# Masking the turned attention probabilities: four VectorE products on the unsplit values, or eight GpSimd products on the two rounded parts

## The chip, the cores and the metric

The kernel runs on one core of one Trainium2 chip. The metric is the device time of one execution in microseconds (us). The engines of a core work beside each other, each through its own list of instructions in order, and meet at semaphores: TensorE (PE) multiplies matrices into PSUM, VectorE (DVE) and ScalarE (ACT) do elementwise work on SBUF and PSUM, GpSimd (POOL) does elementwise work on SBUF, and SyncE (SP) issues transfers.

## The reference, cut to what matters

One decoder layer on 2048 tokens of 1024 channels. A normalised input is projected once into 50 column tiles of 128. One group of columns feeds a short convolution, the other feeds sliding-window attention with 16 heads of 64 in blocks of 128 queries; both are gated, joined, projected back and added to the input. The part that the change touches is the product of the probabilities and the values. A block of queries sees its own 128 keys and the block before, but within a window of 128 in all:

```python
    dist = BLOCK + qi[:, None] - kj[None, :]
    valid = ((dist >= 0) & (dist < WINDOW))[None, :, :] & (key_pos >= 0)[:, None, :]
    ...
    scores = jnp.where(valid[None, :, None, None], scores + alibi[None, None], -jnp.inf)
    ...
    p = jnp.exp(scores - m)
    denom = jnp.sum(p, axis=-1, keepdims=True) + jnp.exp(sink - m)
    probs = (p / denom).astype(v.dtype)
    out = jnp.einsum("bnhgqk,bnkhd->bnqhgd", probs, v_band)
```

So each query has exactly 128 valid keys out of 256: key column k belongs either to the query's own block (k at or before the query) or to the block before it (k after the query). The two sets of valid places are two triangles that fill one 128 x 128 square.

## The kernel before

**Tiles.** The 2048 tokens are two halves of 1024. Within a half, after the key and value columns, a loop runs over 8 tiles of channels; a tile holds two attention heads and 128 convolution channels. A tile has six weight tiles (Q, C, U, B, GC, GA), each multiplied with two chunks of 512 tokens: 12 jobs of 24 matmuls (L1260), since every fp32 operand is split in a rounded part ("hi") and a rest ("lo") and three of the four products are made. There are 16 tiles in all (8 in each half). Behind them comes the output projection (L1427).

**Units.** The attention of a tile is done in 4 units (u = 0 to 3) of two blocks of queries and two heads. Through a unit the work runs so:

- PE `scores(u)` (L1350) into `score_bank`.
- DVE `maxima(u)` (L1009 to L1020): adds the bias, takes row maxima, and folds the two key blocks of a query into one 128 x 128 square by a maximum (L1015), since each place has one valid value only. It begins by waiting for `pT_ready` of unit u-2 (for u = 0: of the unit just before).
- ACT `exps(u)` (L688, L692), DVE `denominators(u)` (L1026, L1028), POOL `normalise(u)` (L512).
- PE `turn(u)` (L1363): four 128 x 128 transposes into `turn_bank`.
- DVE `pT_rest(u)` and ACT `pT_round(u)`: four products of the turned square with the two triangles of `in_block` (L1036) unfold it back into the two key blocks, in the SBUF tile `probs` under its other name `parted`; ACT rounds each query block to `pT_hi` (L701); DVE subtracts to get `pT_lo` (L1042) and signals `pT_ready`.
- PE `weigh(u)` (L1377): 8 matmuls of the values with `pT_hi` and `pT_lo`. It waits for all of `pT_ready` of its unit.
- ACT `shift(u)` (L708, L709) and DVE `attn_out(u)` (L1055) take the result from `out_bank` to `attn_y`.

**Order.** Every engine's order is written out by hand. PE's order in a tile is: Q0, Q1, scores 0, C0, C1, scores 1, U0, turn 0, U1, scores 2, B0, weigh 0, turn 1, GC0, scores 3, GA0, weigh 1, turn 2, B1, GC1, weigh 2, turn 3, GA1, weigh 3. So between turn(u) and weigh(u) stand two jobs for u = 0, 1 and 2, but one (GA1) for u = 3.

DVE's order behind turn(0) is: convolve(0), pT_rest(0), the split of a weight tile (L822), maxima(2), denominators(2), times_b(0) (L1081), convolve(1), attn_out(0), pT_rest(1), gate(GC,0) (L1089), apply_gate (L1097), maxima(3), denominators(3), gate(GA,0), attn_out(1), apply_gate, pT_rest(2), times_b(1), a weight split, gate(GC,1), apply_gate, a weight split, attn_out(2), pT_rest(3), gate(GA,1), attn_out(3), apply_gate. POOL's order in a tile is `normalise` 0 to 2, the squares of the convolution result (`add_squares`, L519 and L522, two instructions each), normalise(3), and three more `add_squares`.

## Time and profile before

| | |
|---|---|
| median of 3 runs | 1688.5 us (1688.47 to 1691.25) |
| profiled execution, span | 1689.7 us |
| PE busy | 1638.5 us, 97% |
| DVE busy | 1038.0 us, 61% |
| ACT busy | 560.3 us, 33% |
| POOL busy | 267.0 us, 16% |

The span is the time from the first to the last instruction of one profiled execution; it lies inside the spread of the runs and 1.2 us above their median. Busy shares are averages over the whole run. In the tile loops they hide that an engine with a low share can still end a wait; what a change there is worth is read from one tile's timeline, and the tiles repeat.

### The profile page before, as it was taken

Reading aid. Unit: us, or ns where it says so; the run is one execution under the profiler, and the core shown is the slowest. Engines: PE = TensorE matmul, PEld = TensorE weight load, DVE = VectorE, ACT = ScalarE, POOL = GpSimd, SP = SyncE. Lnnn points to the kernel's source line nnn. Section 1 sums busy time; section 2 is a strip of 40 time slices with the busy share of each in tenths; the row PEclk is TensorE's granted clock in tenths of the full one; section 3 lists DMA queues with packets and bytes.
Section 4 is the critical chain, followed back from the end, with each engine's and each line's share of the span. In section 5 each row is a group of like instructions: output and inputs, shape, how many; then the busy total and the mean of one; then the engine's idle time right before and its main releaser. Section 6 shows DMA issues by size and latency. Waiting matters only on the chain.

```text
span 1689.7 us, 23074 instructions
## 1 busy us (share of the span) xinstructions
PE 1638.5 (97%) x7824; PEld 1370.7 (81%) x7824; DVE 1038.0 (61%) x2262; ACT 560.3 (33%) x1275; POOL 267.0 (16%) x229
## 2 busy tenths in 40 slices
PE   5999999999999998999999999999999899999996
PEld 4888888888888886788888888888888688888885
DVE  6376767667576758567667676766667643333332
ACT  6333433343333354333333333333333421111110
POOL 1021212122121302112122121312122000000000
...
DMA packets 61774, 125.42 MB, mean 74 GB/s; under 512 B 4640, under 2 KB 37408, under 8 KB 59680
## 3 DMA queue, kind: packets, MB, share of 16 engines
...
## 4 chain that ended last, share of the span: by engine, by line
PE 84%; DVE 8%; issue 3%; ACT 3%; DMA 1%; SPq 0%; DVEq 0%; POOL 0%; ACTq 0%; POOLq 0%
PE job_bank L1260 57%; PE job_bank L1427 8%; PE score_bank L1427 5%; PE turn_bank L1427 5%; PE score_bank L1350 3%; PE out_bank L1377 3%; PE out_bank L1427 2%; DVE probs L1036 1%; PE turn_bank L1363 1%; DVE w_lo L822 1%; DVE hT_lo L857 1%; DVE tanh_sb L1089 1%; DVE pT_lo L1042 1%; ACT pT_hi L701 1%; DVE attn_y L1055 1%
## 5 line engine op out<-in xcount | busy, mean ns | idle before, releaser
L1260 PE MATMUL job_bank<-hT_hi,w_hi 128*128 128x512 f32 x1600 | 635.4, 397 | 9.9 <-DVE conv_y L1081 4.5
L1260 PE MATMUL job_bank<-hT_lo,w_hi 128*128 128x512 f32 x1600 | 627.7, 392 | 0.0
L1260 PE MATMUL job_bank<-hT_hi,w_lo 128*128 128x512 f32 x1600 | 627.7, 392 | 0.0
L1260 PEld LDWEIGHTS job_bank<-hT_hi,w_hi 128*128 128x128 f32 x1600 | 302.9, 189 | 70.2 <-issue 6.0
L1260 PEld LDWEIGHTS job_bank<-hT_hi,w_lo 128*128 128x128 f32 x1600 | 302.6, 189 | 65.5
L1260 PEld LDWEIGHTS job_bank<-hT_lo,w_hi 128*128 128x128 f32 x1600 | 303.2, 190 | 58.5
L512 POOL TENSOR_TENSOR probs<-probs,smax 128x512 f32<-128x512 f32 x64 | 66.6, 1040 | 795.6 <-DVE smax L1028 795.6
L688 ACT ACTIVATE probs<-probs,smax 128x128 f32<-128x128 f32 x256 | 99.8, 391 | 253.4 <-DVE smax L1020 253.4
L822 DVE TENSOR_TENSOR w_lo<-w_raw,w_hi 128x1024 fp32r<-128x1024 f32 x100 | 122.4, 1224 | 87.1 <-ACT w_hi L558 84.3
L701 ACT ACTIVATE pT_hi<-probs 128x512 fp32r<-128x512 f32 x128 | 80.7, 633 | 258.7 <-DVE probs L1036 257.0
L558 ACT ACTIVATE w_hi<-w_raw 128x1024 fp32r<-128x1024 f32 x100 | 105.3, 1053 | 0.8
L793 ACT ACTIVATE wo_raw<-z 128x1024 f32<-128x1024 f32 x16 | 17.0, 1061 | 255.8 <-DVE z L1226 255.8
L1009 DVE CUSTOM_DVE_ANT_0 probs<-score_bank,bias 128x256 f32<-128x256 f32 x256 | 93.0, 420 | 0.7 <-DVE tanh_sb L1089 0.2
L1036 DVE TENSOR_TENSOR probs<-turn_bank,in_block 128x256 f32<-128x256 f32 x256 | 90.8, 418 | 2.0
L1042 DVE TENSOR_TENSOR pT_lo<-probs,pT_hi 128x512 fp32r<-128x512 f32 x128 | 86.8, 696 | 6.8 <-ACT pT_hi L701 4.1
L1026 DVE TENSOR_TENSOR smax<-smax 128x4 f32<-128x4 f32 x64 | 10.4, 163 | 114.2 <-ACT smax L692 114.2
L1427 PE MATMUL job_bank<-wo_early,mix_hi 128*128 128x512 f32 x256 | 69.8, 395 | 7.2 <-DVE wo_early L887 7.2
L1350 PEld LDWEIGHTS score_bank<-keys,qs 128*128 128x128 f32 x512 | 69.5, 188 | 5.5
L1089 DVE SCALAR_TENSOR_TENSOR tanh_sb<-tanh_sb,job_bank 128x512 f32<-128x512 f32 x64 | 43.9, 686 | 46.0 <-ACT tanh_sb L719 44.4
L1226 DVE SCALAR_TENSOR_TENSOR z<-job_bank,mix_r,z 128x512 f32<-128x512 f32 x24 | 17.3, 748 | 87.6 <-PE score_bank L1427 86.6
L1350 PE MATMUL score_bank<-keys,qs 128*128 128x256 f32 x512 | 70.9, 280 | 0.0
L519 POOL TENSOR_TENSOR square<-attn_y 128x512 f32<-128x512 f32 x32 | 40.5, 1267 | 171.2 <-DVE attn_y L1055 171.2
...
## 6 DMA issues: line engine op xcount, KB each, us to landing
...
```

What stands on the lines that cost most here:

```text
L512: nc.gpsimd.tensor_tensor(merged, merged, smax[:, u % 2, ROWSUM, :].unsqueeze(2).to_broadcast([P, 4, BLOCK]), ALU.mult).then_inc(probs_rea ...
L558: nc.scalar.activation(w_hi[:, slot], w_raw[:, slot], ACT.Copy).then_inc(w_hi_ready, 1)
L688: nc.scalar.activation(probs[:, u % 2, c // 2, c % 2, 0:BLOCK], probs[:, u % 2, c // 2, c % 2, 0:BLOCK], ACT.Exp, bias=smax[:, u % 2, NEGM ...
L701: nc.scalar.activation(pT_hi[:, b, :], parted[:, u % 2, b].rearrange("p k h q -> p (k h q)"), ACT.Copy).then_inc(pT_hi_ready, 1)
L822: nc.vector.tensor_tensor(w_lo[:, slot], w_raw[:, slot], w_hi[:, slot].bitcast(F32), ALU.subtract).then_inc(w_ready, 1)
L1009: ins = nc.vector.tensor_tensor_reduce(probs[:, u % 2, h, b, :], score_bank[h][:, b, :], bias[:, first, h, :], 1.0, MASKED, ALU.add, ALU.m ...
L1036: ins = nc.vector.tensor_tensor(parted[:, u % 2, b, kb], turned.rearrange("p (h q) -> p h q", h=2), in_block[:, kb].unsqueeze(1).to_broadc ...
L1042: nc.vector.tensor_tensor(pT_lo[:, b, :], parted[:, u % 2, b].rearrange("p k h q -> p (k h q)"), pT_hi[:, b, :].bitcast(F32), ALU.subtract ...
L1089: nc.vector.scalar_tensor_tensor(out=tanh_sb[:, ch, :], in0=tanh_sb[:, ch, :], scalar=1.0, in1=job_bank[slot][:], op0=ALU.add, op1=ALU.mul ...
L1260: ins = nc.tensor.matmul(job_bank[bank][:], w[:, slot, kt, :], h[:, kt, cols], start=(kt == 0 and n == 0), stop=(kt == KT - 1 and n == 2))
L1350: ins = nc.tensor.matmul(score_bank[h][:, b, :], qs[:, h, blk * BLOCK:(blk + 1) * BLOCK], keys[:, g, part, blk * BLOCK:(blk + 2) * BLOCK], ...
L1427: ins = nc.tensor.matmul(mix_bank[p][s][h], m[:, p, kt, :], wo_part(kt, part)[:, h * CHUNK:(h + 1) * CHUNK], start=(kt % TILES == 0 and n ...
```

## The change

On POOL, a function `part(u)` is new. On ACT, `pT_round(u)` no longer waits for masked values: it waits for the transposes and rounds the unmasked square of both query blocks in one instruction, from `turn_bank` into the first 256 columns of each block of `pT_hi`. On DVE, `pT_rest(u)` is one subtraction, `turn_bank` minus the rounded part, into the same columns of `pT_lo`, and it signals the new `pT_lo_ready`. POOL then waits for that and makes eight products of 128 x 256: for each query block and each of the two parts first the upper triangle into the second 256 columns (signalled by `pT_own`), then, in place, the other triangle onto the first 256 columns, with `pT_ready` behind the last two pairs. All who wait for `pT_ready` (weigh, turn and the start of maxima) thus wait for POOL. Nothing is moved on PE.

```diff
@@ -165,11 +165,11 @@
         gains = sb("gains", [P, 2, TILES])
 
 
-        parted = probs[:].rearrange("p u h b k -> p u (h b k)").rearrange(
-            "p u (b k h q) -> p u b k h q", b=UNIT_BLK, k=2, h=2)
         x_first = [x_sb[:, 0, :], x_sb[:, 1, :]] + [b[:].rearrange("p a b -> p (a b)") for b in (conv_y, gated, c_sb)] + [
             probs[:, i].rearrange("p h b k -> p (h b k)") for i in range(2)] + [
             cu[:, 0:D_MODEL]]
+        hi_parts = pT_hi[:].rearrange("p b (k h q) -> p b k h q", k=2, h=2)
+        lo_parts = pT_lo[:].rearrange("p b (k h q) -> p b k h q", k=2, h=2)
         vT = tanh_sb
         dist = w_raw[:, 2, 0:2, :].bitcast(I32)
         ROWMAX, MAX, NEGMAX, SINKDIFF, ROWSUM, SINKEXP = range(6)
@@ -252,7 +252,8 @@
         rinv_ready = sem("rinv_ready")
         probs_ready = sem("probs_ready")
         probs_turned = sem("probs_turned")
-        masked = sem("masked")
+        pT_lo_ready = sem("pT_lo_ready")
+        pT_own = sem("pT_own")
         pT_hi_ready = sem("pT_hi_ready")
         pT_ready = sem("pT_ready")
         pv_done = sem("pv_done")
@@ -522,18 +523,39 @@
                         nc.gpsimd.tensor_tensor(total[:, ch, :], total[:, ch, :], square[:],
                                                 ALU.add).then_inc(squares_step, 1)
 
+                    def part(u):
+
+                        pool.wait_ge(pT_lo_ready, unit_no(hf, it, u) + 1)
+                        for b in range(UNIT_BLK):
+                            for parts in (hi_parts, lo_parts):
+                                ins = nc.gpsimd.tensor_tensor(
+                                    parts[:, b, 1], parts[:, b, 0].bitcast(F32),
+                                    in_block[:, 1].unsqueeze(1).to_broadcast([P, 2, BLOCK]), ALU.mult)
+                            ins.then_inc(pT_own, 1)
+                        for b in range(UNIT_BLK):
+                            pool.wait_ge(pT_own, 2 * unit_no(hf, it, u) + b + 1)
+                            for parts in (hi_parts, lo_parts):
+                                ins = nc.gpsimd.tensor_tensor(
+                                    parts[:, b, 0], parts[:, b, 0].bitcast(F32),
+                                    in_block[:, 0].unsqueeze(1).to_broadcast([P, 2, BLOCK]), ALU.mult)
+                            ins.then_inc(pT_ready, 1)
+
                     normalise(0)
                     normalise(1)
+                    part(0)
                     normalise(2)
 
                     pool.wait_ge(evacuated[job_slot(hf, it, B, 0)], evac_count(hf, it, B, 0))
                     add_squares(conv_y, ssq_conv, 0, 0)
+                    part(1)
                     normalise(3)
 
                     pool.wait_ge(attn_ready, unit_no(hf, it, 1) + 2)
                     add_squares(attn_y, ssq_attn, 0, 1)
+                    part(2)
                     pool.wait_ge(evacuated[job_slot(hf, it, B, 1)], evac_count(hf, it, B, 1))
                     add_squares(conv_y, ssq_conv, 1, 2)
+                    part(3)
                     pool.wait_ge(attn_ready, unit_no(hf, it, 3) + 2)
                     add_squares(attn_y, ssq_attn, 1, 3)
 
@@ -695,11 +717,10 @@
                     def pT_round(u):
 
                         act.wait_ge(pv_done, unit_no(hf, it, u) + 1)
-                        for b in range(UNIT_BLK):
-
-                            act.wait_ge(masked, 2 * unit_no(hf, it, u) + b + 1)
-                            nc.scalar.activation(pT_hi[:, b, :], parted[:, u % 2, b].rearrange("p k h q -> p (k h q)"),
-                                                 ACT.Copy).then_inc(pT_hi_ready, 1)
+                        act.wait_ge(probs_turned, unit_no(hf, it, u) + 3)
+                        nc.scalar.activation(pT_hi[:, :, 0:2 * BLOCK],
+                                             turn_bank[u % 2][:].rearrange("p (b c) -> p b c", b=UNIT_BLK),
+                                             ACT.Copy).then_inc(pT_hi_ready, 1)
 
                     def shift(u):
 
@@ -1029,19 +1050,11 @@
 
                     def pT_rest(u):
 
-                        dve.wait_ge(probs_turned, unit_no(hf, it, u) + 3)
-                        for b in range(UNIT_BLK):
-                            turned = turn_bank[u % 2][:, 2 * b * BLOCK:2 * (b + 1) * BLOCK]
-                            for kb in range(2):
-                                ins = nc.vector.tensor_tensor(
-                                    parted[:, u % 2, b, kb], turned.rearrange("p (h q) -> p h q", h=2),
-                                    in_block[:, kb].unsqueeze(1).to_broadcast([P, 2, BLOCK]), ALU.mult)
-                            ins.then_inc(masked, 1)
-                        for b in range(UNIT_BLK):
-                            dve.wait_ge(pT_hi_ready, 2 * unit_no(hf, it, u) + b + 1)
-                            nc.vector.tensor_tensor(pT_lo[:, b, :],
-                                                    parted[:, u % 2, b].rearrange("p k h q -> p (k h q)"),
-                                                    pT_hi[:, b, :].bitcast(F32), ALU.subtract).then_inc(pT_ready, 1)
+                        dve.wait_ge(pT_hi_ready, unit_no(hf, it, u) + 1)
+                        nc.vector.tensor_tensor(pT_lo[:, :, 0:2 * BLOCK],
+                                                turn_bank[u % 2][:].rearrange("p (b c) -> p b c", b=UNIT_BLK),
+                                                pT_hi[:, :, 0:2 * BLOCK].bitcast(F32), ALU.subtract
+                                                ).then_inc(pT_lo_ready, 1)
 
                     def attn_out(u):
 
```

On POOL, behind the second normalisation of a tile, there stand before:

```order
L512 TENSOR_TENSOR probs<-probs,smax 128x4x128 [waits rinv_ready]
L529 REGISTER_ALU
L518 ISA [waits evacuated1]
L519 TENSOR_TENSOR square<-conv_y 128x512 [waits squares_step]
L521 REGISTER_ALU
L522 TENSOR_TENSOR ssq_conv<-ssq_conv,square 128x512 [waits squares_step]
```

The row at L512 is normalise(2), and the squares of the convolution follow it. In the changed kernel, from part(0) to normalise(2), with rows that repeat left out:

```order
L531 TENSOR_TENSOR pT_hi<-pT_hi,in_block 128x256 [waits pT_lo_ready]
L531 TENSOR_TENSOR pT_lo<-pT_lo,in_block 128x256
...
L536 ISA
L538 TENSOR_TENSOR pT_hi<-pT_hi,in_block 128x256 [waits pT_own]
L538 TENSOR_TENSOR pT_lo<-pT_lo,in_block 128x256
L536 REGISTER_ALU
...
L511 REGISTER_ALU
L513 TENSOR_TENSOR probs<-probs,smax 128x4x128 [waits rinv_ready]
```

Eight products now stand ahead of normalise(2), and as many ahead of normalise(3), and ahead of and behind the second squares of the convolution.

On DVE, behind the first convolution of a tile, there stand before (the last row is the first instruction of maxima(2)):

```order
L1036 TENSOR_TENSOR probs<-turn_bank,in_block 128x256 [waits probs_turned,dve_step]
L1036 TENSOR_TENSOR probs<-turn_bank,in_block 128x256 x3
L1041 REGISTER_ALU
L1042 TENSOR_TENSOR pT_lo<-probs,pT_hi 128x512 [waits pT_hi_ready] x2
L821 REGISTER_ALU
L822 TENSOR_TENSOR w_lo<-w_raw,w_hi 128x1024 [waits w_hi_ready]
L1002 REGISTER_ALU [waits probs_turned,scores_done,bias_set]
L1009 ISA probs,smax<-score_bank,bias 128x256 [waits pT_ready]
```

In the changed kernel the same place is:

```order
L1054 TENSOR_TENSOR pT_lo<-turn_bank,pT_hi 128x2x256 [waits pT_hi_ready,dve_step]
L842 REGISTER_ALU
L843 TENSOR_TENSOR w_lo<-w_raw,w_hi 128x1024 [waits w_hi_ready]
L1023 REGISTER_ALU [waits probs_turned,scores_done,bias_set]
L1030 ISA probs,smax<-score_bank,bias 128x256 [waits pT_ready]
```

Six instructions have become one. The wait of maxima for `pT_ready` stands where it stood; its signal came from two rows further up on the same engine and now comes from POOL.

## Rows read from the trace of the kernel before

**Rows 1.** The page, part 1: engine, busy us (share), instructions.
```profile
PE 1638.5 (97%) x7824; PEld 1370.7 (81%) x7824; DVE 1038.0 (61%) x2262; ACT 560.3 (33%) x1275; POOL 267.0 (16%) x229
```

**Rows 2.** Busy times over one tile: stretch, length, engines, clock, DMA share, GB/s.
```profile
326.00:401.30 75.30, 75.21 (x370) 63.23 (x369) 52.20 (x120) 26.73 (x70) 15.69 (x12) 1.00 0.17 56
```

**Rows 3.** PE's timeline: start us, us, instruction; first matmuls of weigh 0 to 3.
```profile
325.92 0.28 PE L1377 MATMUL out_bank<-pT_hi,vals 128*128 128x256 f32 x1
...
339.22 0.28 PE L1377 MATMUL out_bank<-pT_hi,vals 128*128 128x256 f32 x1
...
351.53 0.28 PE L1377 MATMUL out_bank<-pT_hi,vals 128*128 128x256 f32 x1
...
358.16 0.39 PE L1260 MATMUL job_bank<-hT_hi,w_lo 128*128 128x512 f32 x1
358.63 0.39 PE L1377 MATMUL out_bank<-pT_hi,vals 128*128 128x256 f32 x1
...
401.23 0.28 PE L1377 MATMUL out_bank<-pT_hi,vals 128*128 128x256 f32 x1
```

**Rows 4.** Waits of the weight loads: us in total, times, longest us.
```profile
PEld out_bank L1377 <- DVE pT_lo L1042: 7.1, 14, 0.5
```

**Rows 5.** DVE's timeline in the same tile, at the places that the change touches.
```profile
318.02 1.42 DVE L1036 TENSOR_TENSOR probs<-turn_bank,in_block 128x256 f32<-128x256 f32 x4
...
321.09 1.23 DVE L822 TENSOR_TENSOR w_lo<-w_raw,w_hi 128x1024 fp32r<-128x1024 f32 x1 [0.26 <-ACT w_hi L558]
322.23 0.42 DVE L1009 CUSTOM_DVE_ANT_0 probs<-score_bank,bias 128x256 f32<-128x256 f32 x1
...
333.06 1.42 DVE L1036 TENSOR_TENSOR probs<-turn_bank,in_block 128x256 f32<-128x256 f32 x4
...
337.37 0.42 DVE L1009 CUSTOM_DVE_ANT_0 probs<-score_bank,bias 128x256 f32<-128x256 f32 x1
...
344.14 1.51 DVE L1097 SCALAR_TENSOR_TENSOR gated<-attn_y,gains,tanh_sb 128x512 f32<-128x512 f32 x1 [0.24 <-DVE attn_y L1055]
345.68 1.42 DVE L1036 TENSOR_TENSOR probs<-turn_bank,in_block 128x256 f32<-128x256 f32 x4
...
353.08 0.75 DVE L1097 SCALAR_TENSOR_TENSOR gated<-conv_y,gains,tanh_sb 128x512 f32<-128x512 f32 x1
...
355.76 1.42 DVE L1036 TENSOR_TENSOR probs<-turn_bank,in_block 128x256 f32<-128x256 f32 x4
```

**Rows 6.** POOL's timeline in the same tile: the squares of attention.
```profile
344.06 1.04 POOL L519 TENSOR_TENSOR square<-attn_y 128x512 f32<-128x512 f32 x1 [0.86 <-DVE attn_y L1055]
345.18 1.62 POOL L522 TENSOR_TENSOR ssq_attn<-ssq_attn,square 128x512 f32<-128x512 f32 x1
```

**Rows 7.** Instructions by line and form: count | busy us, mean ns | idle before.
```profile
L512 POOL TENSOR_TENSOR probs<-probs,smax 128x512 f32<-128x512 f32 x64 | 66.6, 1040 | 795.6 <-DVE smax L1028 795.6
L481 POOL TENSOR_SCALAR_AFFINE_SELECT in_block<-in_block 128x128 f32<-128x128 f32 x1 | 0.3, 292 | 0.0
L1036 DVE TENSOR_TENSOR probs<-turn_bank,in_block 128x256 f32<-128x256 f32 x256 | 90.8, 418 | 2.0
L1042 DVE TENSOR_TENSOR pT_lo<-probs,pT_hi 128x512 fp32r<-128x512 f32 x128 | 86.8, 696 | 6.8 <-ACT pT_hi L701 4.1
L857 DVE TENSOR_TENSOR hT_lo<-score_bank,hT_hi 128x512 fp32r<-128x512 f32 x14 | 9.0, 685 | 2.0 <-ACT hT_hi L569 1.9
L569 ACT ACTIVATE hT_hi<-score_bank 128x512 fp32r<-128x512 f32 x14 | 7.7, 592 | 6.5 <-PE score_bank L1281 6.5
```

**Rows 8.** Stretches of 4 us between the halves, columns as in Rows 2.
```profile
640.00:644.00 4.00, 1.76 (x8) 1.13 (x6) 3.87 (x8) 2.92 (x4) 0.00 (x0) 1.00 0.00 0
...
652.00:656.00 4.00, 1.72 (x12) 1.31 (x10) 3.79 (x11) 1.35 (x3) 3.36 (x3) 1.00 0.20 58
656.00:660.00 4.00, 1.80 (x4) 1.49 (x5) 3.97 (x6) 2.18 (x4) 2.17 (x2) 0.61 0.42 139
660.00:664.00 4.00, 4.00 (x11) 3.11 (x10) 3.93 (x4) 0.00 (x0) 1.57 (x2) 0.53 0.00 0
```

## The prediction

> **What bounds the kernel now.** I read the busy shares first: PE is busy for 1638.5 of 1689.7 us, DVE for 61%, ACT and POOL far less [rows 1]. So a shorter DVE is worth something only where PE waits for it. Next one tile: from the first matmul of weigh(0) in one tile to the same in the next is 401.23 - 325.92 = 75.31 us [rows 3], and in such a stretch PE is busy for 75.21 us [rows 2]. PE sets the pace of all 16 tiles and is nearly full; what is to be found is where it waits in them, and what could make it wait more. It waits in one place: in front of weigh(3). The last matmul of the job GA1 starts at 358.16, the next could follow 0.23 later at 358.39, and weigh(3) starts at 358.63 [rows 3]. That is 0.24 us; the waits of the weight loads name DVE's pT_lo, 14 times, 0.5 us at most [rows 4]. So the chain behind turn(3) already ends last by a hair, with only one job as cover. The other weighs have two jobs as cover and start without a wait.
>
> **The change part by part.**
>
> DVE loses four products of 418 ns each [rows 7]. Since each starts before the last has ended, four take from 318.02 to about 319.5. It also loses one of two subtractions of 696 ns; the one left reads PSUM and is nearest to the split of the input, 685 ns [rows 7]. Per unit that is some 1.45 + 0.65 = 2.1 us less. ACT loses one rounding; the one that is left reads PSUM like the rounding of the input, 592 ns [rows 7], and can run as soon as the transposes are in, while DVE is still at other things. In units 0 to 2 it is hidden behind those; in unit 3 it runs beside attn_out(2). Taken alone these are worth the 0.24 us per tile.
>
> POOL gains eight products per unit. No 128x256 product is in the trace. Bounds per product: the 128x512 product of normalise takes 1040 ns [rows 7], so 1.04 us from above (no shrinking at all); 0.29 us from below, since a 128x128 select with one input takes 292 ns [rows 7]. I take 0.55 us, half of the 1040 ns and a little for what doesn't shrink. A run of eight is then 4.4 us, where DVE's own part took 2.8 us and ACT's ran inside it. The new run is not hidden by DVE's saving: it lies in series behind the subtraction.
>
> The second cost is a collision. POOL's square at 344.06 ran for 1.04 us; DVE's apply_gate, started at 344.14 with both inputs in SBUF, took 1.51 us, against 0.75 us for the same shape at 353.08 [rows 5, 6]. The other way round, POOL's next instruction of the same size took 1.62 us beside that apply_gate [rows 6]. So the two engines take turns: a DVE instruction with two SBUF inputs costs a POOL run most of its own length (for the weight split of 1.23 us at 321.09 [rows 5] I take 1.05 us, for apply_gate 0.55 us: 1.62 - 1.04, rounded).
>
> The third cost is the wait that stays in front of maxima. maxima(2) waits for unit 0 and maxima(3) for unit 1. That was free when DVE itself signalled `pT_ready`; now DVE, in order, stands still until POOL's run has ended, and with it all that is queued behind: exps, times_b, convolve, attn_out and the next subtraction. Worked through in the tile of [rows 3, 5, 6], with 0.68 us for a subtraction:
>
> - Unit 0. The subtraction runs at 318.02 to 318.7. POOL's run: 318.7 + 4.4 + 1.05 (a weight split falls into it) = 324.15. weigh(0) is due at 325.92: no stall. But maxima(2), which began at 322.23, begins at 324.15: DVE is 1.9 us later from here.
> - Unit 1. The subtraction starts at 333.06 + 1.9 = 335.0 and ends at 335.7. Run: + 4.4 + 0.55 = 340.65. weigh(1) is due at 339.22: **a stall of 1.4 us**. maxima(3) moves from 337.37 to 340.65: DVE is 3.3 us late.
> - Unit 2. The subtraction starts at 345.68 + 3.3 = 349.0. POOL must first end its squares, which ended at 345.18 + 1.62 = 346.8 and now end at 350.1. Run: 4.4, one weight split (1.05), apply_gate (0.55), and a second split that falls on the run's end; I count half of it (0.5): 356.6. weigh(2) is due at 351.53 + 1.4 = 352.9: **a stall of 3.7 us**.
> - Unit 3. weigh(2) starts at 356.6, so weigh(3) is due 358.39 - 351.53 = 6.86 us later, at 363.45. weigh(2) and turn(3) need 1.3 us; shift (0.8), attn_out (0.9) and the subtraction (0.7) follow weigh(2)'s 0.95: 359.95. Run: 364.35. **Stall 0.9 us**, 0.7 more than before.
>
> Sum: 1.4 + 3.7 + 0.7 = 5.8 us per tile, 93 us for 16. I add nothing for the half boundary, where DVE is busy for 3.87 and 3.97 of 4 us while PE idles for some of it [rows 8]: there DVE's saving of up to 8 us per tile and POOL's added latency pull against each other. The profiled span is 1689.7 us, 1.2 above the median; the sum, made on its rows, is added to the median: 1688.5 + 93 = 1781.5 us.
>
> The Trainium skill, SBUF: State Buffer, section "SBUF: two separate sides", calls the port pair of DVE and GpSimd an exclusive lock that whichever starts first holds for the whole instruction. By that rule every product of the run is a separate taking of the lock, and the collisions above are paid in full; the rows have it for single POOL instructions, none shows a run of eight. Were it to let a waiting DVE instruction in only when the run is over, the stalls of weigh(1) and weigh(2) would shrink, that of weigh(3) would grow, and the sum would stay near 5 to 6 us.
>
> **The rivals.**
>
> *Slower, but by the last unit alone.* If collisions cost little in short products, unit 1's run ends before 339.22 and DVE's 2.1 us per unit absorb the waits of maxima. What then stays is unit 3: before, attn_out(2) ended at about 355.75, where the masks began [rows 5]; subtraction until 356.45, run until 360.85, due at 358.39. That is 2.46, less the 0.24 of before: 2.2 us per tile, 36 us in all, **1724 us**. For it: the POOL instructions of the trace that collide are twice as long as the new ones. Against it: the rows that show the collisions. Chance 0.2.
>
> *Longer products.* At 0.70 us a run is 1.2 us longer, and it counts at units 0, 1, 2 and 3 in series: 5.8 + 4.8 = 10.6 us per tile, **1858 us**. For it: POOL's second squares took 1.62 us. Against: that was a collision, and 0.70 is far above half of 1040 ns. Chance 0.1.
>
> *PE's clock falls.* PE idled for 2.3 us of the stretch at 652 and 2.2 us of the next, one gap of 4.5 us at most; the granted clock was 1.00 up to there and then 0.61 and 0.53 over 8 us, so stretches at the lower of the two levels, 1.2 GHz in place of 2.4; the loss is 4 x 0.39 + 4 x 0.47 = 3.4 us. In the stretch at 640, with 2.2 us of idling in it, it stayed 1.00 [rows 8]. My 3.7 us in front of weigh(2) lies between. Should it fall there in each tile, 3.4 us are lost, of which the 0.9 us of weigh(3) come back, since the slower GA1 covers more: 2.5 x 16 = 40 us more, **1821 us**. The Trainium skill, TensorE: Matmul & The Clock Gate, section "Part 1: The HAM clock gate", has the gate pass half the pulses once PE has been idle; by it the stall in front of weigh(2) is the one to watch. Chance 0.15.
>
> *Faster.* Should a product take less than (358.39 - 356.45) / 8 = 0.24 us, POOL is done before every weigh is due and DVE's relief stays: 0.24 x 14 = 3.4 us, and some 4.5 us of the idling at 640 and 656, where DVE is full: **1680 us**. Only its sign is other; its price needs products shorter than a one-input select of half their columns, 292 ns [rows 7]. At about 0.25 to 0.27 us the time would not change. Chance 0.02, and 0.02 for no change.
>
> **How the numbers follow.** The forecast, with products of 0.50 to 0.60 us and collisions paid, has 0.51; in it a tile is longer by 4.5 to 8 us, so 1760 to 1817 us. Then 0.2 for the last unit alone, 0.15 for the clock, 0.1 for longer products, 0.02 and 0.02 for the others. The range must hold eight in ten: it goes from 1722 to 1836 us and leaves out the longer products and the cases without loss. Faster by over 0.2% (about what a measurement of this kernel can tell from no change) has 0.02, within 0.2% 0.02, slower 0.96.
>
> **What would show it.** In the profile of the changed kernel: POOL's busy time rises by 512 x 0.57, some 290 us, to about 560 us and more where products collide; DVE's falls to about 900 us. PE's waits name POOL in front of the matmuls of weigh, 16 times each for units 1, 2 and 3, some 1.4, 3.7 and 0.9 us each, none for unit 0. DVE waits for POOL in front of the maxima. Tiles come every 81 us. The granted clock stays 1.00 inside the tiles. Wrong if: the waits are in front of weigh(3) alone (then collisions are cheap); the products' start-to-start is far from 0.55 us; or the clock falls behind each long stall.

## The result and the profile after

The changed kernel takes 1869.28 us (median of 4 runs, 1864.32 to 1871.19), the kernel before on the same chip 1689.11 us. The ratio is 1.1058, with a 95% interval of 1.1044 to 1.1072: 180 us slower. The profiled execution's span is 1869.6 us. The forecast was 1781.5 us with a range of 1722 to 1836, so the sign was right and the time lies above the range, nearest to the rival "longer products" (1858 us, chance 0.1).

The busy times on the page of the changed kernel, which answer to [rows 1]:

```profile
PE 1705.1 (91%) x7824; PEld 1420.0 (76%) x7824; DVE 940.9 (50%) x1942; ACT 521.2 (28%) x1211; POOL 669.1 (36%) x741
```

DVE loses 97 us, ACT 39 us, and POOL gains 402 us where I expected some 290. PE does the same 7824 matmuls, and has 67 us more of busy time: some of them ran at the lower clock.

The waits of the changed kernel (engine, line, who was waited for; us in total, times, longest), which answer to [rows 4]:

```profile
PEld out_bank L1390 <- POOL pT_lo L538: 148.0, 49, 6.3
PE out_bank L1390 <- POOL pT_lo L538: 127.7, 48, 5.9
DVE probs L1030 <- POOL pT_lo L538: 124.6, 32, 5.0
```

PE waits for POOL's last product (L538) in front of `weigh` 48 times: 47 times at units 1, 2 and 3 (in the last tile weigh(2) doesn't wait) and once, for 4.9 us, in front of weigh(0) at the half boundary. DVE waits for the same product in front of maxima (L1030) 32 times, two per tile. Apart from that one weigh(0) these are the places that the prediction named; their sizes are the question.

One tile on PE, the first matmul of each weigh (start us, us, instruction, idle before and releaser), which answers to [rows 3]:

```profile
271.21 0.28 PE L1390 MATMUL out_bank<-pT_hi,vals 128*128 128x256 f32 x1
...
288.42 0.58 PE L1390 MATMUL out_bank<-pT_hi,vals 128*128 128x256 f32 x1 [3.75 <-POOL pT_lo L538]
...
304.58 0.39 PE L1390 MATMUL out_bank<-pT_hi,vals 128*128 128x256 f32 x1 [2.17 <-POOL pT_lo L538]
...
357.01 0.28 PE L1390 MATMUL out_bank<-pT_hi,vals 128*128 128x256 f32 x1
```

weigh(3) of this tile starts at 314.37. In the table the four intervals of a tile stand side by side; the row "worked out" is the prediction's, from its stalls of 1.4, 3.7 and 0.7 us.

| | weigh 0 to 1 | 1 to 2 | 2 to 3 | 3 to the next 0 | tile |
|---|---|---|---|---|---|
| before | 13.30 | 12.31 | 7.10 | 42.60 | 75.31 |
| worked out | 14.7 | 16.0 | 7.8 | 42.6 | 81.1 |
| changed, this tile | 17.21 | 16.16 | 9.79 | 42.64 | 85.80 |

Two of the 15 intervals from tile to tile lie around the half boundary and are longer for that; of the other 13, ten are between 85.66 and 85.99 us, and three have 1.3 to 2.9 us more in the last interval, two of them also 1.2 us more in the one before (tiles of 87.0 to 89.8 us). Against 75.31 us that is 10.4 us per tile, 166 of the 180 us for 16 tiles; the rest is in those three tiles, around the half boundary and in the last tile (45.3 us from weigh(0) to weigh(3), for 32.5).

POOL in this tile, unit 1's run and parts of the runs of units 2 and 3 (start us, us, instruction):

```profile
282.39 0.74 POOL L531 TENSOR_TENSOR pT_hi<-pT_hi,in_block 128x256 fp32r<-128x256 f32 x1 [3.24 <-DVE pT_lo L1054]
283.08 0.74 POOL L531 TENSOR_TENSOR pT_lo<-pT_lo,in_block 128x256 fp32r<-128x256 f32 x1
283.78 1.18 POOL L531 TENSOR_TENSOR pT_hi<-pT_hi,in_block 128x256 fp32r<-128x256 f32 x1
284.93 0.72 POOL L531 TENSOR_TENSOR pT_lo<-pT_lo,in_block 128x256 fp32r<-128x256 f32 x1
...
287.65 0.72 POOL L538 TENSOR_TENSOR pT_lo<-pT_lo,in_block 128x256 fp32r<-128x256 f32 x1
...
297.96 0.74 POOL L531 TENSOR_TENSOR pT_hi<-pT_hi,in_block 128x256 fp32r<-128x256 f32 x1
298.66 1.72 POOL L531 TENSOR_TENSOR pT_lo<-pT_lo,in_block 128x256 fp32r<-128x256 f32 x1
...
308.74 0.73 POOL L531 TENSOR_TENSOR pT_hi<-pT_hi,in_block 128x256 fp32r<-128x256 f32 x1 [0.54 <-DVE pT_lo L1054]
```

A product that meets nothing takes 0.72 to 0.74 us and the next starts 0.69 us later, not 0.55. The one at 283.78 met apply_gate (283.25) and took 0.46 us more; the one at 298.66 met the weight split (298.29) and took 1.0 us more. Unit 1's run goes from 282.39 to 288.37, and weigh(1) starts at 288.42; unit 2's goes from 297.96 to 304.52, and weigh(2) starts at 304.58; unit 3's goes from 308.74 to 314.31, and weigh(3) starts at 314.37. Three times in the tile the end of POOL's run is what PE starts on. DVE's maxima start on it as well, at 270.88 and 288.56, the second after 4.18 us of idling.

The clock in the same tile (stretch, length, busy us of PE, PEld, DVE, ACT, POOL, then the granted clock, DMA share, GB/s):

```profile
288.00:292.00 4.00, 3.58 (x15) 3.43 (x16) 2.46 (x12) 0.88 (x5) 0.36 (x1) 0.57 0.00 0
292.00:296.00 4.00, 4.00 (x19) 3.29 (x18) 2.54 (x6) 2.71 (x10) 1.78 (x2) 1.00 0.00 0
304.00:308.00 4.00, 3.42 (x15) 3.23 (x16) 3.94 (x5) 1.35 (x3) 3.92 (x3) 0.65 0.20 66
```

Behind PE's idle gap of 3.75 us in front of weigh(1), and again behind the one of 2.17 us in front of weigh(2), a part of the stretch ran at the lower of the two levels. The forecast had 1.00 throughout.

Behind weigh(1) the lower clock lasts longer in some tiles. In the 8 us behind it the mean is 0.79 to 0.82 in 11 of the 13 tiles away from the half boundary, but 0.62 and 0.63 in the other two, those of 88.2 and 89.8 us. The tile that starts at 357.01 (weigh(1) at 374.22, weigh(2) at 390.40, weigh(3) at 401.28), PE's clock first and then DVE's last weight split ahead of attn_out(2) (L1068), beside the same split in the tile above:

```profile
374.00:378.00 4.00, 3.78 (x15) 3.59 (x16) 2.46 (x12) 1.07 (x5) 0.17 (x1) 0.50 0.00 0
378.00:382.00 4.00, 4.00 (x15) 3.18 (x14) 2.73 (x6) 2.51 (x9) 1.98 (x2) 0.72 0.00 0
...
391.82 2.31 DVE L843 TENSOR_TENSOR w_lo<-w_raw,w_hi 128x1024 fp32r<-128x1024 f32 x1
394.05 0.85 DVE L1068 TENSOR_TENSOR attn_y<-out_bank,o_shift 64x256 f32<-64x256 f32 x2
...
305.00 2.06 DVE L843 TENSOR_TENSOR w_lo<-w_raw,w_hi 128x1024 fp32r<-128x1024 f32 x1
307.08 0.86 DVE L1068 TENSOR_TENSOR attn_y<-out_bank,o_shift 64x256 f32<-64x256 f32 x2
```

With PE's jobs late, this split ends 3.73 us behind weigh(2) in place of 2.48, POOL's run for unit 3 starts 5.30 us behind it in place of 4.05 to 4.37, and weigh(3) waits for 3.75 us.

### The profile page after: what moved, and what is told of

Read it like the earlier page. It is cut to its first block, busy times and chain, and to the rows that moved or that the text cites. A ratio compares the mean times of both kernels' runs of the same rounds, so it can differ in the third digit from the quotient of the medians.

```text
span 1869.6 us, 23125 instructions
## 1 busy us (share of the span) xinstructions
PE 1705.1 (91%) x7824; PEld 1420.0 (76%) x7824; DVE 940.9 (50%) x1942; ACT 521.2 (28%) x1211; POOL 669.1 (36%) x741
## 4 chain that ended last, share of the span: by engine, by line
PE 44%; POOL 25%; issue 18%; DVE 7%; ACT 5%; DMA 1%; POOLq 0%; DVEq 0%; SPq 0%; ACTq 0%
PE job_bank L1273 22%; PE job_bank L1440 7%; POOL pT_lo L531 6%; POOL pT_lo L538 5%; PE score_bank L1440 5%; PE turn_bank L1440 4%; POOL pT_hi L538 3%; POOL pT_hi L531 3%; POOL square L520 3%; POOL ssq_conv L523 3%; ACT probs L710 2%; DVE probs L1030 2%; PE out_bank L1440 2%; PE out_bank L1390 2%; POOL probs L513 1%
## 5 line engine op out<-in xcount | busy, mean ns | idle before, releaser
L1273 PE MATMUL job_bank<-hT_hi,w_hi 128*128 128x512 f32 x1600 | 649.2, 406 | 4.3 <-DVE hT_lo L878 4.3
L1273 PE MATMUL job_bank<-hT_lo,w_hi 128*128 128x512 f32 x1600 | 637.0, 398 | 0.0
L1273 PEld LDWEIGHTS job_bank<-hT_hi,w_hi 128*128 128x128 f32 x1600 | 311.9, 195 | 66.2 <-issue 4.9
L513 POOL TENSOR_TENSOR probs<-probs,smax 128x512 f32<-128x512 f32 x64 | 66.6, 1040 | 591.3 <-DVE smax L1049 591.3
L1390 PE MATMUL out_bank<-pT_hi,vals 128*128 128x256 f32 x256 | 85.3, 355 | 127.7 <-POOL pT_lo L538 127.7
L843 DVE TENSOR_TENSOR w_lo<-w_raw,w_hi 128x1024 fp32r<-128x1024 f32 x100 | 140.6, 1406 | 114.5 <-ACT w_hi L580 112.1
L1390 PEld LDWEIGHTS out_bank<-pT_hi,vals 128*128 128x128 f32 x256 | 60.2, 235 | 148.6 <-POOL pT_lo L538 148.0
L1030 DVE CUSTOM_DVE_ANT_0 probs<-score_bank,bias 128x256 f32<-128x256 f32 x256 | 93.2, 421 | 125.1 <-POOL pT_lo L538 124.6
L531 POOL TENSOR_TENSOR pT_hi<-pT_hi,in_block 128x256 fp32r<-128x256 f32 x128 | 103.9, 812 | 119.9 <-DVE pT_lo L1054 119.9
L531 POOL TENSOR_TENSOR pT_lo<-pT_lo,in_block 128x256 fp32r<-128x256 f32 x128 | 126.2, 986 | 0.0
L1102 DVE SCALAR_TENSOR_TENSOR tanh_sb<-tanh_sb,job_bank 128x512 f32<-128x512 f32 x64 | 43.9, 685 | 123.0 <-ACT tanh_sb L740 121.4
L538 POOL TENSOR_TENSOR pT_hi<-pT_hi,in_block 128x256 fp32r<-128x256 f32 x128 | 95.9, 750 | 0.0
L538 POOL TENSOR_TENSOR pT_lo<-pT_lo,in_block 128x256 fp32r<-128x256 f32 x128 | 94.1, 735 | 0.0
L740 ACT ACTIVATE tanh_sb<-job_bank 128x512 f32<-128x512 f32 x64 | 37.9, 592 | 188.8 <-PE job_bank L1273 182.7
L1068 DVE TENSOR_TENSOR attn_y<-out_bank,o_shift 64x256 f32<-64x256 f32 x128 | 53.9, 421 | 52.3 <-ACT o_shift L730 50.9
```

The costliest lines, as they stand in the source:

```text
L513: nc.gpsimd.tensor_tensor(merged, merged, smax[:, u % 2, ROWSUM, :].unsqueeze(2).to_broadcast([P, 4, BLOCK]), ALU.mult).then_inc(probs_rea ...
L531: ins = nc.gpsimd.tensor_tensor(parts[:, b, 1], parts[:, b, 0].bitcast(F32), in_block[:, 1].unsqueeze(1).to_broadcast([P, 2, BLOCK]), ALU. ...
L538: ins = nc.gpsimd.tensor_tensor(parts[:, b, 0], parts[:, b, 0].bitcast(F32), in_block[:, 0].unsqueeze(1).to_broadcast([P, 2, BLOCK]), ALU. ...
L843: nc.vector.tensor_tensor(w_lo[:, slot], w_raw[:, slot], w_hi[:, slot].bitcast(F32), ALU.subtract).then_inc(w_ready, 1)
L1030: ins = nc.vector.tensor_tensor_reduce(probs[:, u % 2, h, b, :], score_bank[h][:, b, :], bias[:, first, h, :], 1.0, MASKED, ALU.add, ALU.m ...
L1273: ins = nc.tensor.matmul(job_bank[bank][:], w[:, slot, kt, :], h[:, kt, cols], start=(kt == 0 and n == 0), stop=(kt == KT - 1 and n == 2))
```

## The experiments

Their order here follows the questions, and the interval is always from the first matmul of one weigh to that of the next.

**What one product costs.** In the kernel before, ahead of the first tile, POOL makes products of many forms on scratch tiles, each waiting for the one ahead; the kernel's own work is untouched. The one run took 1688.39 us, so nobody waited for them.

```diff
+                    for _ in range(3):
+                        then(nc.gpsimd.tensor_tensor(fold(half, 2), fold(src[:, 0:256], 2), two, ALU.mult))
...
+                        then(nc.gpsimd.tensor_tensor(square[:, 0:256], src[:, 0:256], other[:, 0:256], ALU.mult))
+                        then(nc.gpsimd.tensor_tensor(fold(square[:, 0:256], 2), fold(src[:, 0:256], 2), ident[:, 0:2].unsqueeze(2).to_broadcast([P, 2, BLOCK]), ALU.mult))
...
+                        then(nc.gpsimd.tensor_tensor(square[:, 0:128], src[:, 0:128], other[:, 0:128], ALU.mult))
```

> The kernel before, with ten forms of GpSimd product run alone, three times each and one after the other, in the stretch ahead of the tile loops where VectorE makes few instructions (their results are not used). It prices the product by itself. Theory A (two different full operands are slow, 2.15 ns per column, since the adding of squares, 128x512 with two different tensors, never took under 1271 ns, and squares of one tensor or products with a repeated scalar took 1040): 128x256 with in_block or another tensor 0.72 us, with a repeated scalar about 0.53; 128x512 1.27 and 1.04; rounded output and writing in place change nothing. Theory B (rounded output, or in place, is slow): only those forms take 0.72, the others 0.53. The time is 1688 to 1695 us, since no one waits for the forms.

POOL's timeline of that kernel, first round of the forms:

```profile
42.52 0.73 POOL L522 TENSOR_TENSOR pT_hi<-pT_hi,in_block 128x256 fp32r<-128x256 f32 x1
...
45.03 0.73 POOL L524 TENSOR_TENSOR square<-attn_y 128x256 f32<-128x256 f32 x1
45.84 0.61 POOL L525 TENSOR_TENSOR square<-attn_y,ident 128x256 f32<-128x256 f32 x1
...
47.90 1.29 POOL L527 TENSOR_TENSOR square<-attn_y 128x512 f32<-128x512 f32 x1
49.27 1.04 POOL L528 TENSOR_TENSOR square<-attn_y,ident 128x512 f32<-128x512 f32 x1
50.39 0.46 POOL L529 TENSOR_TENSOR square<-attn_y 128x128 f32<-128x128 f32 x1
```

L524, L527 and L529 multiply two different tiles (the row names both halves of `attn_y` once); L525 and L528 have one tile and a scalar repeated along it. With two different full operands the time is 0.46, 0.73 and 1.29 us for 128, 256 and 512 columns, which is 0.18 us and 2.15 ns per column. With a repeated scalar it is 0.61 and 1.04 us. Rounding the output, working in place or taking the mask made no difference (0.73 to 0.74 us). These are the prices of products that met nothing; each form was made three times, and some of the 30 products took up to 1.0 us more (1.63 us for the one at 43.32, left out above). So the 1040 ns of normalise [rows 7], which multiplies by a repeated scalar, was the price of a cheaper form. The dearer form stands in the trace of before as well: the sums of the squares add two different tiles. Their line in that kernel, with the least, the median and the longest ns and the starts of the first and the last:

```profile
L522 POOL TENSOR_TENSOR ssq_conv<-ssq_conv,square x32: 1272/1324/1355, 103.2 to 1304.3; 128x512 f32<-128x512 f32 x32
L522 POOL TENSOR_TENSOR ssq_attn<-ssq_attn,square x32: 1271/1618/1629, 119.5 to 1319.4; 128x512 f32<-128x512 f32 x32
```

Not one of 64 takes less than 1271 ns. I had one of them at 1.62 us in [rows 6] and put all above 1040 ns down to the collision. The Trainium skill, GPSIMD Engine Reference, section "3.1 Elementwise — side-by-side cycle accounting", has GpSimd read two operands in turns and gives 4497 ns for an add over 2048 columns. An estimate from that figure is 2.2 ns per column; the runs here agree with 2.15.

**Fewer and wider products.** Four products of 128x512 in place of eight of 128x256.

```diff
-                        for b in range(UNIT_BLK):
-                            for parts in (hi_parts, lo_parts):
-                                ins = nc.gpsimd.tensor_tensor(
-                                    parts[:, b, 1], parts[:, b, 0].bitcast(F32),
...
+                        for parts in (pT_hi, pT_lo):
+                            nc.gpsimd.tensor_tensor(
+                                parts[:, :, 256:512].rearrange("p b (h q) -> p b h q", q=BLOCK),
```

> The changed kernel with four products of 128x512 per unit (both query blocks in one instruction) in place of eight of 128x256; the same elements are multiplied. Theory (each GpSimd product has a large fixed part, since a 128x256 takes 0.69 us from start to start and the 128x512 of normalise 1.00): four take 1.0 us each, a run falls from 5.6 to 4.1 us, and the kernel to 1695 to 1750 us. Rival (products of two full operands, or with rounded output, are slow per element, 2.7 ns): four take 1.4 us each, a run stays at 5.5 us, and the time stays at 1850 to 1870 us.

1849.14 us, ratio 1.095 (1.0917 to 1.0984). An undisturbed product took 1.25 to 1.29 us, twice the narrow one less 0.15 to 0.2 us. The price is by column and not by instruction, and the number of products was not what made them dear; four instructions fewer per unit gave back 20 us.

**Half of the products.** Only `pT_hi` is masked; the first columns of `pT_lo` stay unmasked and the others zero.

```diff
+            nc.gpsimd.memset(pT_lo[:, :, 2 * BLOCK:].bitcast(F32), 0.0)
...
-                            for parts in (hi_parts, lo_parts):
+                            for parts in (hi_parts,):
```

> The changed kernel in which GpSimd masks only the rounded part pT_hi, four products in place of eight; pT_lo is left unmasked in its first columns and zero in the others. Theory (the run's length behind the subtraction is the cause of everything, the clock's fall included): a run is 2.8 us as long as VectorE's part was before, all stalls but some 0.5 to 1 us in front of weigh(3) go, and the time is 1690 to 1710 us. Rival (the split of work over one more engine and its signals cost by themselves): over 1730 us.

1700.36 us in the one run made, with intervals of 13.30, 12.31, 7.96 and 42.6. With runs of half the length weigh(1) and weigh(2) start without a wait, and only unit 3 is late, by 0.86 us per tile. The structure of the new chain isn't dear in itself: what is dear is its length against the cover of two jobs.

**The same eight products, shorter.** They multiply by a column of ones, repeated, which is the cheaper form; nothing is masked.

```diff
-                                    in_block[:, 1].unsqueeze(1).to_broadcast([P, 2, BLOCK]), ALU.mult)
+                                    ones[:].unsqueeze(2).to_broadcast([P, 2, BLOCK]), ALU.mult)
...
-                                    in_block[:, 0].unsqueeze(1).to_broadcast([P, 2, BLOCK]), ALU.mult)
+                                    ones[:].unsqueeze(2).to_broadcast([P, 2, BLOCK]), ALU.mult)
```

> The changed kernel in which the eight products multiply by a repeated scalar (a column of ones) in place of in_block: as many, of the same shape, in the same places, but nothing is masked. It puts the product at the duration of which the forecast was made. If a 128x256 product takes 0.50 to 0.55 us here, the forecast's other steps stand or fall alone: they gave 1781 us, with intervals between the weighs of 14.7, 16.0 and 7.8 us. Theory (the price of the product was the failed term, the rest was right): 1765 to 1800 us. Rival (the chain behind a unit has another part that is longer than worked out): over 1810 us. If the product is no faster here, the run says nothing.

1819.41 us, ratio 1.0769 (1.0753 to 1.0785). The product took 0.61 us, 0.57 start to start, nearly the price that I had used, and yet the time is 38 us above my sum: the price alone, worth 50 us, does not explain the miss. Most tiles alternate between 84.6 and 82.6 us. Three stretches of a tile of the first kind and one of the second:

```profile
282.00:284.00 2.00, 2.00 (x12) 1.77 (x11) 1.93 (x10) 0.00 (x0) 0.00 (x0) 0.72 0.00 0
284.00:286.00 2.00, 2.00 (x6) 1.56 (x5) 0.17 (x2) 1.96 (x10) 0.00 (x0) 0.50 0.00 0
...
307.00:309.00 2.00, 2.00 (x9) 1.81 (x8) 0.00 (x0) 0.54 (x2) 0.00 (x0) 0.50 0.00 0
...
382.00:384.00 2.00, 2.00 (x12) 2.00 (x11) 0.62 (x1) 0.41 (x2) 1.92 (x2) 0.50 0.42 131
```

weigh(1) had started at 281.34 behind 1.83 us of idling, weigh(3) at 306.48 behind 2.84 us, and in the other tile weigh(2) at 381.60 behind 3.06 us. Behind each of them the clock was at the lower level for some us.

**The clock, in that kernel.** PE makes matmuls whose result nobody reads in front of its wait.

```diff
-                        pe.wait_ge(pT_ready, 2 * unit_no(hf, it, u) + 4)
...
+                        for n in range(0 if last and hf == 1 else {1: 8, 2: 12}.get(u, 0)):
+                            nc.tensor.matmul(out_bank[:].rearrange("p b h q -> p (b h q)"), keys[:, 0, 0, BLOCK:2 * BLOCK],
+                                             keys[:, 0, 0, BLOCK:BLOCK + CHUNK], start=True, stop=True)
+                        pe.wait_ge(pT_ready, 2 * unit_no(hf, it, u) + 4)
```

> The changed kernel with the products by the column of ones (0.57 us start to start; nothing is masked), and PE makes 8 matmuls of 512 columns in front of its wait for POOL in weigh(1) and 12 in weigh(2), into a bank that weigh then writes anew; their values are not used. In the kernel with short products alone the tiles alternate: in one the gap of 1.83 us in front of weigh(1) is followed by a clock of 0.72, 0.50 and 0.93 over 6 us and the one of 2.84 us in front of weigh(3) by 0.50 and 0.71, and the tile takes 84.6 us; in the other the gap of 3.08 us in front of weigh(2) is followed by 0.50 and 0.68, and the tile takes 82.6 us. Theory, the clock is what that kernel costs above the 1781 us that I had worked out for a product of this length: with the gaps filled the clock stays at 1.00 behind weigh(1) and weigh(2), weigh(3) starts 8 to 8.4 us behind weigh(2) in place of 9.1 to 10, each tile takes 81.2 to 81.9 us, and the time is 1778 to 1795 us. Rival, as in the fill of the changed kernel, the jobs behind weigh(1) end earlier and POOL's run for unit 2 meets more of DVE's instructions: 1810 us or above.

1792.45 us, ratio 1.0613 (1.0588 to 1.0638): 27 us less than without the filling. The first stretch below begins just behind the start of weigh(2) (292.93), the second holds the start of weigh(3) (301.36):

```profile
293.00:297.00 4.00, 4.00 (x24) 3.54 (x25) 2.49 (x4) 1.35 (x3) 3.45 (x3) 1.00 0.22 66
...
301.00:305.00 4.00, 3.64 (x20) 3.19 (x21) 1.86 (x4) 2.04 (x3) 0.80 (x2) 1.00 0.00 0
```

The clock stays at 1.00, and every tile inside a half but those next to the boundary takes 81.93 to 81.98 us, with intervals of 15.28, 15.64, 8.42 and 42.6. My worked-out tile has 81.1 us, and with 0.57 in place of 0.55 us for 32 products 81.7. So with the right price and an unbroken clock the sum of a tile holds, though its terms don't each: with 0.57 us I would have 15.0, 16.2 and 8.0, so the first interval is 0.3 and the third 0.5 us longer than worked out and the second 0.5 us shorter. That they cancel is luck.

**The clock, in the changed kernel.** The same filling with 16 matmuls in front of weigh(1) and 8 in front of weigh(2), the products untouched.

```diff
+                        for n in range(0 if last and hf == 1 else {1: 16, 2: 8}.get(u, 0)):
```

> The changed kernel with TensorE kept at work in its waits: 16 matmuls of 128x512 whose result is overwritten stand in front of the wait of weigh(1) and 8 in front of that of weigh(2), about 3.6 and 1.8 us where it stood still for 3.9 and 2.2 us. Theory (3.4 us of each tile are the granted clock's fall to 0.57 and 0.65 behind the two gaps): the clock stays at 1.00 in the tiles, a tile comes down from 85.7 to 82 to 83 us, the kernel to 1805 to 1830 us. Rival (the clock falls for another reason, or the time behind the gaps has another cause): no gain, 1865 to 1880 us.

1882.33 us, ratio 1.1147 (1.1103 to 1.1191): slower by 13 us, so the gain that I expected didn't come. The clock did stay at 1.00 behind weigh(1). Behind weigh(2) it still fell (0.58 in the 4 us from 396.90), since PE waited there for another 3.3 us with its 8 matmuls done; so this run tests an unbroken clock at weigh(1) only. With it the jobs behind weigh(1) end earlier, and POOL's run for unit 2 meets more of DVE's work:

```profile
389.49 1.71 POOL L531 TENSOR_TENSOR pT_lo<-pT_lo,in_block 128x256 fp32r<-128x256 f32 x1
...
393.25 1.25 POOL L538 TENSOR_TENSOR pT_lo<-pT_lo,in_block 128x256 fp32r<-128x256 f32 x1
394.47 1.70 POOL L538 TENSOR_TENSOR pT_hi<-pT_hi,in_block 128x256 fp32r<-128x256 f32 x1
```

The first met a weight split (DVE, 389.11), the second apply_gate (393.17), the third the next split (393.84). The run takes 8.0 us where it took 6.56, and the interval 17.6 where it was 16.16. In the changed kernel the slow clock behind weigh(1) had cost nothing in the interval that follows, since POOL's chain and not PE ended it (16.14 to 16.18 us in all 13 tiles away from the boundary, with a mean clock of 0.62 as with 0.82); it had even kept two collisions away.

**Maxima without the wait.** In the changed kernel the turned probabilities no longer pass through `probs`, whose reuse this wait guarded, so it can go.

```diff
-                        dve.wait_ge(pT_ready, 2 * unit_no(hf, it, u) + (2 if u == 0 else 0))
```

> The changed kernel without the wait of maxima for pT_ready (the maxima overwrite nothing that the changed pT_rest still reads). Theory: of the 10.4 us that a tile has gained, one part is the series run(0) - maxima(2) - run(1) - maxima(3) - run(2), since VectorE stands still 124.6 us in front of the maxima. Then the stall in front of weigh(2), 2.2 us, goes, that of weigh(1) shrinks from 3.9 to 1.5 to 2.5 us, that of weigh(3) may grow; a tile comes down from 85.7 to 78 to 81 us, the kernel to 1740 to 1790 us. Rival (only the length of each run counts, the maxima's waits cost nothing): 1860 to 1870 us.

1829.56 us, ratio 1.0834 (1.08 to 1.0869), 40 us less than the changed kernel and between the two expectations. The intervals are 15.5, 12.9, 11.1 and 43.9 to 45.4 in all but one of the tiles away from the boundary. weigh(1) loses 1.7 of its 3.9 us and weigh(2) nearly all, but weigh(3) now waits for 4.0 us more than before, and the clock falls behind it: 0.64 in the stretch from 307 to 311, which costs 1.3 to 2.8 us of each last interval. A part of what the wait cost only moved to the last unit.

**Both at once**, short products and no wait of maxima (the two edits shown above together).

> The changed kernel with both changes at once that were tried apart: the products multiply by the column of ones (0.57 us start to start; nothing is masked, so the output is another) and maxima doesn't wait for POOL. Apart, the shorter product took off 50 us (1869 to 1819) and the wait 40 us (1869 to 1830). Theory, the two are separate costs (a run's length counts at each unit, the wait makes DVE late from unit to unit): they add up, 1869 - 50 - 40 = 1779 us, between 1770 and 1790; the interval from weigh(0) to weigh(1) falls from 15.3 to about 14.5 us. Rival, they are one cost seen twice (the wait costs something only because the run is long): the time stays above 1800 us.

1743.44 us, ratio 1.0331 (1.0301 to 1.0361). Neither held: the two together took off 126 us and not 90. The intervals are 13.74, 12.40, 9.83 and, in 9 of the 13 tiles away from the boundary, 42.6. PE's timeline at weigh(3):

```profile
291.25 0.39 PE L1388 MATMUL out_bank<-pT_hi,vals 128*128 128x256 f32 x1 [2.79 <-POOL pT_lo L538]
```

POOL's run ahead of it goes from 286.60 to 291.20, undisturbed. This is the rival "by the last unit alone": it gave 2.2 us per tile, here it is 2.7 and some 0.5 at unit 1. Either cure alone leaves gaps long enough for the clock to fall; both together leave only the one in front of weigh(3), behind which it falls in four of those 13 tiles. That fits the sign of the 36 us that are left over; I haven't split them further.

**Unit 0 alone on POOL**, the others masked on DVE as before, and maxima without the wait.

```diff
+                    on_pool = (0,)
...
+                        if u not in on_pool:
+                            return
...
-                    part(3)
...
-                        dve.wait_ge(pT_ready, 2 * unit_no(hf, it, u) + (2 if u == 0 else 0))
```

> GpSimd masks unit 0 of each tile only, as in the changed kernel, without a wait of the maxima for it; units 1 to 3 are masked on VectorE as before. Theory (what costs is the run of 5.6 to 6.6 us where the cover is too short; unit 0 has the most cover, some 7.2 us from its subtraction to weigh(0)): no stall in front of weigh(0), tiles of 75.3 us, and 1683 to 1690 us; VectorE's relief of 2.1 us in a tile is worth at most 3 us, at the half boundary. Rival (collisions with the weight split make the run longer than the cover): tiles of 75.5 to 77 us, 1693 to 1715 us.

1700.93 us, ratio 1.0071 (1.0056 to 1.0087). Even at the unit with the widest cover the run took 7.0 us, with collisions of 1.0 and 0.46 us in it; it ended at 326.95, and weigh(0) started on it at 327.00. That costs less than 0.1 us, though. A tile takes 75.89 us, 0.58 more than before, and 0.43 of it lies between weigh(2) and weigh(3) (7.53 for 7.10), where PE waits for DVE:

```profile
360.23 0.39 PE L1425 MATMUL out_bank<-pT_hi,vals 128*128 128x256 f32 x1 [0.51 <-DVE pT_lo L1090]
```

DVE is late from unit 0 on: beside POOL's run its maxima(2) start at 323.04, and three instructions of them take 1.13, 0.70 and 0.67 us where they take 0.69, 0.16 and 0.17 in the kernel before. At pT_rest(1) and pT_rest(2) it is 1.0 us nearer to its weigh than before. Moving one unit out of four is a loss too, and by these rows more through what POOL's run does to DVE than through its length; no run tests the two apart.

**The wait in front of weigh(3), in the kernel before.** ACT's and DVE's sixth weight split of a tile moves behind pT_round(3) and pT_rest(3); nothing else changes.

```diff
-                    split_next(5)
...
+                    split_next(5)
```

> The kernel before with the last weight split of a tile moved behind pT_rest(3) on VectorE and behind pT_round(3) on ScalarE. Theory (TensorE's one wait in a tile, 0.24 us in front of weigh(3), is the chain shift(2), attn_out(2), pT_rest(3), held up by the split of 1.2 us ahead of it): the wait goes, tiles of 75.07 in place of 75.31 us, 3 to 4 us less, 1685 us. Rival (the weight tile comes later and the next load with it, so that the third job of the next tile waits): 1690 to 1700 us.

1686.64 us (11 runs) against 1688.99 (15 runs), ratio 0.9984 (0.9975 to 0.9993). The first matmul of weigh(3), which in [rows 3] waited for 0.24 us:

```profile
356.43 0.40 PE L1260 MATMUL job_bank<-hT_hi,w_lo 128*128 128x512 f32 x1
356.67 0.28 PE L1377 MATMUL out_bank<-pT_hi,vals 128*128 128x256 f32 x1
```

It starts 0.24 us behind the job's last matmul, so the wait is gone and a tile takes 74.97 us, 0.34 less. By 16 tiles 5.4 us were to be had; the median moved by 2.4. In the profiled execution the interval across the half boundary is 1.2 us longer (127.45 for 126.25), which takes back a part. It is the fastest version of this study, by a margin as small as what can be told from no change.

**The same move with POOL's products**, once in the kernel with short products and once in the changed kernel.

> The kernel of x5_cheap (products with a repeated scalar, nothing is masked) with the last weight split of a tile moved behind pT_rest(3) and pT_round(3), as in y2_move. In x5_cheap the interval from weigh(2) to weigh(3) was 9.1 and 10.0 us by turns where 7.8 had been worked out, and the trace showed attn_out(2) queued behind a weight split of 2.31 us that had collided with GpSimd's squares. Theory (that queue is the missing 1.3 to 2.2 us): 7.6 to 8.4 us for the interval, a run(2) without the split's collision, tiles of 79.5 to 81 us, 1765 to 1795 us. Rival (the interval is long because of TensorE's lower clock or of ScalarE's part): stays over 9 us, 1810 us or more.

1822.4 us, ratio 1.0777 (1.0739 to 1.0816), against 1819.41 without the move. In the tile that I followed weigh(2) ran at the lower clock (2.07 us for its matmuls) and ACT's shift, which waits for them, began only at 300.13, so a split out of the way helped nobody, and the moved split then met POOL's run. In the tiles of the kind whose interval from weigh(2) to weigh(3) was 9.96 us it did help (POOL's run starts 3.75 us behind weigh(2) and not 5.3), and the collision takes two thirds of that back: the interval is 9.4 us.

> The changed kernel, whole, with the same split moved. There run(2) ended so late that the split lay ahead of weigh(2) or beside the squares, and attn_out(2) did not wait for it: the interval from weigh(2) to weigh(3) was 9.7 us with ScalarE's shift as the last to come. Theory: the move changes little there, 9.5 to 9.7 us for the interval, tiles of 85 to 86 us, 1850 to 1870 us. Rival (the split costs the changed kernel over 1 us per tile): below 1850 us.

1881.73 us, ratio 1.1128 (1.1085 to 1.1172), 12 us slower than the changed kernel. Both expectations missed it. Its timeline has DVE's moved split and, right behind, the first product of unit 3's run:

```profile
309.52 1.23 DVE L843 TENSOR_TENSOR w_lo<-w_raw,w_hi 128x1024 fp32r<-128x1024 f32 x1
309.61 1.73 POOL L531 TENSOR_TENSOR pT_hi<-pT_hi,in_block 128x256 fp32r<-128x256 f32 x1 [1.02 <-DVE pT_lo L1054]
```

Behind the subtraction is the one place in the tile where POOL's run is sure to be under way, and the product pays the split's length of 1.0 us. What helps where DVE itself masks costs 0.7 us per tile where POOL does (interval 2 to 3 of 10.37 for 9.69). That is about half of the 12 us. The other half is the clock: behind weigh(3) it falls (0.57 to 0.69 over 4 us) in eight of the 13 tiles away from the boundary, and the last interval is 44.0 to 44.2 us there, where the changed kernel has three such tiles.

## Why the prediction was right in its places and wrong in its size

The forecast's steps, each with what the runs showed:

- **DVE's and ACT's relief**: worth nothing, as expected. DVE's busy time falls by 97 us where I had some 138 (1038 to about 900), since its splits and gates now meet POOL's products (100 splits take 1406 ns on average, for 1224 before; the one at 298.29 takes 1.50 us, 1.23 us in [rows 5]); and DVE spends 124.6 us waiting for POOL.
- **The price of a product, 0.55 us: the step that failed.** I took half of normalise's 1040 ns "and a little for what doesn't shrink". Two things were wrong in it: normalise multiplies by a repeated scalar, which is a cheaper form, and the part that doesn't shrink is 0.18 us. It is 0.69 us start to start and 5.55 us for a run in place of 4.4. Of the 88 us between forecast and result, 50 are the step from 0.69 to 0.57 us (1869 to 1819), and another 10, worked out as 32 x 0.02 us x 16, are the step to 0.55. The rival with 0.70 us gave 1858, and I gave it 0.1 with the reason that 0.70 was "far above half of 1040 ns": the same wrong reading once more.
- **The collisions**: right in price. 1.05 and 0.55 us were taken, 1.0 and 0.46 were measured, in the middle of a run as for single instructions. They are paid in full, one after the other. The 0.55 came out right by luck, though: it was 1.62 - 1.04, and the undisturbed form of that 1.62 us row takes 1.27 us, so the collision in [rows 6] was 0.35 us. It is the misread price once more. In number they were fewer in unit 2: one split, where I had counted a split, apply_gate and half of another.
- **Unit 0**: right. weigh(0) starts without a wait. But maxima(2) start only 0.33 us ahead of it (270.88), where I had 1.77 us: the run is 1.15 us longer, starts 0.1 us later, and the maxima begin 0.2 us behind its end and not with it.
- **Unit 1, 1.4 us**: it is 3.9. The 1.44 us of unit 0, passed on by the wait of maxima, and 1.03 us of a longer run (5.98 for 4.95) are the 2.5 us between.
- **Unit 2, 3.7 us**: it is 3.85, and right for the wrong reason. The run takes 6.56 us, where I had 4.4 and 2.1 of collisions; it is 5.55 and 1.0. The products' price and the collisions' number were off by the same amount in opposite directions, which is luck.
- **Unit 3, 0.7 us**: it is 2.6. Of it 1.15 are the longer run. Another 0.8 us come ahead of it: POOL's run starts 4.16 us behind weigh(2) and not 3.35. Half of that is my chain being too short: in the kernel with the gaps filled, where neither clock nor split is in the way, the run starts 3.75 us behind weigh(2) (1.30 us to ACT's shift, where I had 0.95). Some 0.3 us are the weight split on DVE, which I had counted with unit 2's run and not here: it ends 2.48 us behind weigh(2), and in the tiles where the shift starts at 1.30 the run still starts at 4.05. Only the last 0.1 us goes with the clock, at which weigh(2)'s matmuls ran in part (until 306.17).
- **The clock stays at 1.00**: wrong. It fell behind the gaps of 3.75 and 2.17 us. I had it as a rival behind weigh(2) only, and as an alternative to longer products, when longer products make the gaps that let it fall. It costs 27 us in the kernel with short products (1819 to 1792). In the changed kernel it costs nothing between weigh(1) and weigh(2), up to 0.3 us in front of weigh(3) in most tiles, 1.2 us there in the two tiles where it stayed low for longer, and 1.3 to 2.9 us behind weigh(3) in three tiles. By these rows the 13 tiles away from the boundary are together 8.6 us longer than 13 of the common 85.69 us. No run has the changed kernel's products with an unbroken clock and no new collisions, so its share there stays this estimate. The step from the low clock behind weigh(1) to the late weigh(3) shows in the kernel with short products: its seven tiles with a mean of 0.72 over the 6 us behind weigh(1) have POOL's run 5.30 us behind weigh(2), the six with 1.00 have it at 4.4 to 4.6, and with the gaps filled it is at 3.75 in all 13.
- **The serialising wait of maxima**: right as a mechanism. Without it and with short products the stalls of weigh(1) and weigh(2) are all but gone, 1743 for 1819 us.
- **Nothing for the half boundary**: a small miss. The interval from the last tile of the first half to the first of the second is 132.5 us and the one ahead of it 94.7, against 126.3 and 75.3. Together they are 25.6 us longer where two tiles inside a half are 20.8. There weigh(0) does wait for POOL, for 4.9 us. I didn't take that stretch apart.

Taken apart in this order the 88 us are 50 (the product's form), 27 (the clock) and 11 (0.57 for 0.55 us, and 1 us left); in another order the shares would differ, as the experiment with both cures shows. In the changed kernel itself the rows show some 9 us that go with the clock, so there most of the 88 us is the length of the runs.
